# A two-layer hybrid decoder trunk in float32: the MLP's first product with its weights standing still, for 13 of 16 chunks

## The reference, cut to what matters

```python
def hybrid_layer(x, c_act, ...):
    mod = c_act @ ada_w + ada_b                 # 2048 -> 6 * 2048
    sh_a, sc_a, gt_a, sh_m, sc_m, gt_m = jnp.split(mod[:, None, :], 6, axis=-1)
    ...                                         # mixers, x = x + gt_a * (o @ w_out)
    h = rms_norm(x, norm_mlp) * (1.0 + sc_m) + sh_m
    u = jnp.square(jax.nn.relu(h @ mlp_w1))     # 256 x 2048 by 2048 x 8192
    return x + gt_m * (u @ mlp_w2)              # 256 x 8192 by 8192 x 2048
```

## Time and profile before

| what | value |
|---|---|
| median of 3 runs (lowest, highest) | 2588.86 us (2587.51, 2595.3) |
| profiled execution, its own time | 2593.14 us |
| its span, first to last instruction | 2591.1 us |
| mean granted TensorE clock | 0.977 |
| MLP of layer 1, supers 1 to 3 | 2043 to 2577 us of the span |
| MLP of layer 0, supers 1 to 3 | 819 to 1370 us |
| HBM read | 629.85 MB, 244 GB/s over the span |

### The profile page before, as it was taken

One profiled execution on the slowest core, in us unless ns is written; L12 is line 12 of the kernel. 1 busy time (PEld: TensorE's weight loads), 2 busy tenths in 40 slices (PEclk: granted clock), 3 DMA queues, 4 the chain that ended last, 5 costly groups with the idle time before them and its releaser, 6 DMA issues.

```text
span 2591.1 us, 29622 instructions
## 1 busy us (share of the span) xinstructions
PE 2403.2 (93%) x11276; PEld 1982.8 (77%) x11276; DVE 1789.3 (69%) x2145; ACT 1183.6 (46%) x1602; POOL 19.3 (1%) x44
## 2 busy tenths in 40 slices
PE   2679899997999999999998998999899999999997
PEld 1567777775887888887887877887788888888886
DVE  6888877767877777778776777676567545545555
ACT  2244554443543544444544555454454454453453
POOL 1000000000000000000000000000000000000000
PEclk9899999998999999999999999999999999999999
DMA  8978776777988989989885787556577666666664
GB/s 301 323 266 275 256 259 212 231 248 246 327 292 305 304 287 317 306 299 309 296 292 190 249 276 253 165 186 219 151 239 261 188 185 193 190 185 195 184 190 138
DMA packets 318549, 633.91 MB, mean 245 GB/s; under 512 B 20365, under 2 KB 41289, under 8 KB 317769
## 3 DMA queue, kind: packets, MB, share of 16 engines
q1 hardware_dynamic: 314368, 625.49, 73.4%
q10 hardware_dynamic: 4040, 6.54, 0.7%
HBM read 629.85 MB, written 2.10 MB: 244 GB/s over the span
## 4 chain that ended last, share of the span: by engine, by line
PE 36%; issue 33%; DVE 18%; DMA 8%; ACT 4%; POOL 0%; ACTq 0%; DVEq 0%; POOLq 0%
PE acc L1500 8%; PE acc L1502 7%; PE acc L1501 7%; DVE ada_acc L998 7%; DMA ada_raw<-in_ada_w 7%; DVE w_lo L1039 5%; PE pair L1500 2%; PE pair L1502 2%; PE pair L1501 2%; ACT w_hi L675 2%; PE bank_T L1411 1%; DMA w_raw<-in_nsa_cmp_v_w 1%; PE bank_T L1373 1%; DVE ybuf L1153 1%; DMA w_raw<-in_nsa_cmp_k_w 1%
## 5 line engine op out<-in xcount | busy, mean ns | idle before, releaser
L1039 DVE TENSOR_TENSOR w_lo<-w_raw,w_hi 128x1024 fp32r<-128x1024 f32 (+3 forms) x828 | 979.9, 1192 | 399.8 <-ACT w_hi L675 398.0
L675 ACT ACTIVATE w_hi<-w_raw 128x1024 fp32r<-128x1024 f32 (+3 forms) x828 | 848.6, 1033 | 795.3 <-PE acc L1502 369.5
L1500 PE MATMUL acc<-w_hi,hT_hi 128*128 128x512 f32 (+3 forms) x1536 | 613.3, 399 | 56.2 <-DVE w_lo L1039 42.6
L1502 PE MATMUL acc<-w_lo,hT_hi 128*128 128x512 f32 (+3 forms) x1536 | 592.8, 386 | 0.0
L1501 PE MATMUL acc<-w_hi,hT_lo 128*128 128x512 f32 (+3 forms) x1536 | 592.7, 386 | 0.0
L998 DVE SCALAR_TENSOR_TENSOR ada_acc<-ada_raw,silu_c,ada_acc 128x1024 f32<-128x1024 f32 x300 | 384.1, 1280 | 113.9 <-DMA ada_raw<-in_ada_w 113.0
L1500 PEld LDWEIGHTS acc<-w_hi,hT_hi 128*128 128x128 f32 x1536 | 294.6, 192 | 121.7 <-issue 31.3
L1502 PEld LDWEIGHTS acc<-w_lo,hT_hi 128*128 128x128 f32 x1536 | 293.6, 191 | 57.1
L1501 PEld LDWEIGHTS acc<-w_hi,hT_lo 128*128 128x128 f32 x1536 | 294.9, 192 | 51.7 <-issue 1.2
L1500 PE MATMUL acc<-w_hi,uT_hi 128*128 128x512 f32 (+1 forms) x720 | 284.9, 396 | 3.5 <-DVE w_lo L1039 3.5
L1502 PE MATMUL acc<-w_lo,uT_hi 128*128 128x512 f32 (+1 forms) x720 | 280.3, 389 | 0.0
(11 more groups left out here) (240 smaller groups left out, 2029.2 us busy)
## 6 DMA issues: line engine op xcount, KB each, us to landing
w_raw<-in_mlp_w SPq DMA_DIRECT2D x512, 512.0 KB, 4.8
ada_raw<-in_ada_w SPq DMA_DIRECT2D x320, 512.0 KB, 5.0
w_raw<-in_w_in SPq DMA_DIRECT2D x112, 512.0 KB, 4.9
arena<-in_ada_w SPq DMA_DIRECT2D x64, 512.0 KB, 6.2
w_raw<-in_w_out SPq DMA_DIRECT2D x64, 512.0 KB, 5.0
w_raw<-in_nsa_cmp_k_w SPq DMA_DIRECT2D x32, 512.0 KB, 4.7
w_raw<-in_nsa_cmp_v_w SPq DMA_DIRECT2D x32, 512.0 KB, 4.8
w_raw<-in_w_in SPq DMA_DIRECT2D x16, 388.0 KB, 4.0
```

Source lines behind the costliest of these rows:

```text
L675: a.activation(w_hi[:, Q % RING, :, 0:n], w_raw[:, Q % RING, :, 0:n], ACT.Copy).then_inc(hi_done, 1)
L1039: v.tensor_tensor(w_lo[:, Q % RING, :, 0:n], w_raw[:, Q % RING, :, 0:n], w_hi[:, Q % RING, :, 0:n].bitcast(F32), ALU.subtract).then_inc(lo ...
L1500: pe.matmul(o, st_hi[:, kt + k, tok], wh, start=first and k == 0, stop=False)
L1502: mm = pe.matmul(o, st_hi[:, kt + k, tok], wl, start=False, stop=last and k == 1)
```

## The change

For the chunks (s,0) to (s,3), all but (0,0), (0,1) and (0,2), the roles in the first product are exchanged. 13 chunks a layer, so 26 chunks and 208 pieces. `product_turned` loads 128 columns of the weight tile as TensorE's stationary operand. `w_hi` meets `hT`, one tensor now in which the high and the low input of a row of tiles lie side by side: 512 columns, high by high in the left 256 and low by high in the right. `w_lo` meets only the high input: 256 columns, added to the left. A chunk is worked as two halves t of 256 hidden features, each with an accumulator of its own, so a turned chunk takes two of the three. The sums have features on partitions, and there is no turn.

At a chunk's end ScalarE copies the right halves to `ybuf` (`u_copy`), VectorE adds the left halves from PSUM (`u_sum_halves`), ScalarE does relu, square and the rounding to `uT_hi` (`u_act`), VectorE the low part (`u_low`). The copies and additions stand at the second piece after the chunk's last, the rest at the second to fifth (two later in super 0). TensorE raises `u_pair` from the last matmul of half 0; for half 1 it waits for its own `piece_used` and then raises it. The core of the diff:

```diff
-def acc_of(chunk):
-    return CHUNKS[chunk][3] if type(chunk) is str else (8 * chunk[0] + chunk[1]) % 3
+def turned(chunk):
+    return type(chunk) is not str and chunk[1] < 4 and chunk not in ((0, 0), (0, 1), (0, 2))
...
+        for key in [chunk + (0,), chunk + (1,)] if turned(chunk) else [chunk]:
+            ACC_OF[l, key] = CHUNKS[key][3] if type(key) is str else turn_no % 3
...
+    for s in range(SUPERS):
+        for j in range(4):
+            if turned((s, j)):
+                done = 64 * s + 8 * j + 7
+                for t in range(2):
+                    side(M + done + 2, ("usum", l, s, j, t), 0)
+                    side(M + done + 2 + t + 2 * (s == 0), ("uact", l, s, j, t), 3)
+                    side(M + done + 4 + t + 2 * (s == 0), ("ulo", l, s, j, t), 3)
...
-        hT_hi, hT_lo = sb("hT_hi", [P, KT, SEQ], F32R), sb("hT_lo", [P, KT, SEQ], F32R)
+        hT = sb("hT", [P, KT, 2, SEQ], F32R)
+        hT_hi, hT_lo = hT[:, :, 0, :], hT[:, :, 1, :]
...
+            def u_copy(l, s, j, t):
+                n = U_NO[l, s, j, t]
...
+                act.wait_ge(u_pair, n + 1)
+                a.activation(u_half(j, t), acc[ACC_OF[l, (s, j, t)]][:, :, 256:512], ACT.Copy).then_inc(u_copied, 1)
+
+            def u_act(l, s, j, t):
+                n = U_NO[l, s, j, t]
+                act.wait_ge(u_sum, n + 1)
+                a.activation(u_half(j, t), u_half(j, t), ACT.Relu).then_inc(u_own, 1)
+                act.wait_ge(u_own, 2 * n + 1)
+                a.activation(u_half(j, t), u_half(j, t), ACT.Square).then_inc(u_own, 1)
+                act.wait_ge(u_own, 2 * n + 2)
+                kt = 4 * j + 2 * t
+                a.activation(uT_hi[:, kt:kt + 2, :], u_half(j, t), ACT.Copy).then_inc(v_hi, 1)
...
+            def u_sum_halves(l, s, j, t):
+                n = U_NO[l, s, j, t]
+                dve.wait_ge(u_copied, n + 1)
+                v.tensor_tensor(u_half(j, t), acc[ACC_OF[l, (s, j, t)]][:, :, 0:256], u_half(j, t), ALU.add
+                                ).then_inc(u_sum, 1)
+                dve.wait_ge(u_sum, n + 1)
+                dve.sem_inc(acc_free[ACC_OF[l, (s, j, t)]], 1)
+
+            def u_low(l, s, j, t):
+                kt = 4 * j + 2 * t
+                dve.wait_ge(v_hi, split_value(l, f"u{s}_{2 * j + t}"))
+                v.tensor_tensor(uT_lo[:, kt:kt + 2, :], u_half(j, t), uT_hi[:, kt:kt + 2, :].bitcast(F32), ALU.subtract
+                                ).then_inc(split_done, 1)
...
+            def product_turned(Q):
+                l, chunk, p = PIECES[Q]
+                pe.wait_ge(lo_done, Q + 1)
+                for t in range(2):
+                    key = chunk + (t,)
+                    if p == 0 and ACC_USE[l, key]:
+                        pe.wait_ge(acc_free[ACC_OF[l, key]], ACC_USE[l, key])
+                    for f in range(2):
+                        o = acc[ACC_OF[l, key]][:, f, :]
+                        for k in range(2):
+                            kt, cols = 2 * p + k, slice(P * (2 * t + f), P * (2 * t + f) + P)
+                            pe.matmul(o, w_hi[:, Q % RING, k, cols], hT[:, kt, :, :].rearrange("p a t -> p (a t)"),
+                                      start=p == 0 and k == 0, stop=False)
+                            mm = pe.matmul(o[:, 0:SEQ], w_lo[:, Q % RING, k, cols], hT_hi[:, kt, :], start=False,
+                                           stop=p == 7 and k == 1)
+                    if p == 7 and t == 0:
+                        mm.then_inc(u_pair, 1)
+                mm.then_inc(piece_used, 1)
+                if p == 7:
+                    pe.wait_ge(piece_used, Q + 1)
+                    pe.sem_inc(u_pair, 1)
```

More of the change, by code:

```diff
@@ L80 @@
 assert len(PIECES) == ALL
-def acc_of(chunk):
-    return CHUNKS[chunk][3] if type(chunk) is str else (8 * chunk[0] + chunk[1]) % 3
-LAST_PIECE, ACC_USE = {}, {}
-uses = [0, 0, 0]
+def turned(chunk):
+    return type(chunk) is not str and chunk[1] < 4 and chunk not in ((0, 0), (0, 1), (0, 2))
+LAST_PIECE, ACC_OF, ACC_USE = {}, {}, {}
+uses, turn_no = [0, 0, 0], 0
 for Q, (l, chunk, p) in enumerate(PIECES):
     if p == 0:
-        ACC_USE[l, chunk] = uses[acc_of(chunk)]
-        uses[acc_of(chunk)] += 1
+        if chunk == (0, 0):
+            turn_no = 0
+        for key in [chunk + (0,), chunk + (1,)] if turned(chunk) else [chunk]:
+            ACC_OF[l, key] = CHUNKS[key][3] if type(key) is str else turn_no % 3
+            turn_no += type(key) is not str
+            ACC_USE[l, key] = uses[ACC_OF[l, key]]
+            uses[ACC_OF[l, key]] += 1
     LAST_PIECE[l, chunk] = Q
@@ L231 @@
     side(M + 12, ("fill", l, "n2", 3), 0)
[L232 to L237, removed]
+    u_relu = {(0, 0): 22, (0, 1): 24, (0, 2): 29}
+    u_t = {(0, 0): (22, 23), (0, 1): (25, 26), (0, 2): (30, 31)}
     mlp_steps = []
@@ L345 @@
                                              "fq", "fk"]
-    for i, name in enumerate(names + [f"n2y{j}" for j in range(4)] + [(s, j) for s in range(SUPERS) for j in range(4)]):
+    for i, name in enumerate(names + [f"n2y{j}" for j in range(4)] + [(0, j) for j in range(3)]):
         slot = i % 2 if i < len(names) else (i - len(names)) % 2
@@ L469, in trunk @@
         v_hi, split_done = sem("v_hi"), sem("split_done")
+        u_pair, u_copied, u_sum, u_own = sem("u_pair"), sem("u_copied"), sem("u_sum"), sem("u_own")
         x_done, x_squared = sem("x_done"), sem("x_squared")
@@ L503, in acc_out @@
         def acc_out(l, chunk):
-            return acc_free[acc_of(chunk)], ACC_USE[l, chunk] + 1
+            return acc_free[ACC_OF[l, chunk]], ACC_USE[l, chunk] + 1
         def split_value(l, name):
@@ L808, in evac @@
             def evac(l, name):
-                a_ = acc[acc_of(name)]
+                a_ = acc[ACC_OF[l, name]]
                 if name == "fv":
@@ L889, in after @@
                         relu(l, step[2], step[3])
+                    elif kind == "usum":
+                        u_copy(l, step[2], step[3], step[4])
+                    elif kind == "uact":
+                        u_act(l, step[2], step[3], step[4])
                     elif kind == "square":
@@ L1315, in after @@
                         diagonals(l, step[2])
+                    elif kind == "usum":
+                        u_sum_halves(l, step[2], step[3], step[4])
+                    elif kind == "ulo":
+                        u_low(l, step[2], step[3], step[4])
                     elif kind == "resid":
@@ L1579, in _ @@
                     t_in(l, what)
-                if PIECES[Q][1] == "cw1":
+                if turned(PIECES[Q][1]):
+                    product_turned(Q)
+                elif PIECES[Q][1] == "cw1":
                     compress(Q)
```

36 lines of the change are left out of this document (22 added, 14 removed).

## The result

| | before | changed |
|---|---|---|
| median of 5 runs (lowest, highest) | 2588.86 us (2587.51, 2595.3) | 2606.5 us (2603.84, 2615.49) |
| profiled execution, span | 2593.14, 2591.1 us | 2606.5, 2604.5 us |

The ratio is 1.0075, 95% interval 1.0056 to 1.0094: 0.75% slower, where no difference was forecast and 2606 was the range's end. Run again in a later batch it gave 1.0077 (1.0058 to 1.0096).

The account below looks back on a forecast made before the run. TensorE's queue was taken as the bound, in layer 0 until VectorE or DMA takes over. Terms -25.2 + 11.0 + 10.9 + 5 = +1.7 us gave 2590.6, told as 2591 us; range for 8 in 10: 2578 to 2606.

Parts of the forecast that it names:

- Transposes: TensorE's queue, 26 first-product chunks: the transposes go, 0.97 us a chunk, -25.2 us in all.
- Shape: 208 turned pieces: 8 matmuls of 512 and 8 of 256 columns, 2.774 instead of 2.720 us each, +11.0 us.
- The self-wait: End of each turned chunk: TensorE waits for its own last matmul, 0.42 us a time, +10.9 us; bounds 4 to 14.
- ScalarE's chain: ScalarE's chunk-end work: about 2.7 us extra a chunk, `w_hi` still in time with 0.7 us to spare, 0 in layer 1.
- VectorE: Layer 0's turned chunks: additions fit but leave nothing to make up late landings, 0.4 us a chunk, +5 us; bounds 0, +16.
- rival B: Layer 0's first product: VectorE becomes the bound, additions and low halves ahead of `w_lo`, +16 us, 2605; chance 0.24.
- Accumulators: A turned chunk takes two of three: free in layer 1, in layer 0 part of the 0.4 us a chunk for VectorE.
- The sign for layer 1: Layer 1's turned chunks: the forecast is wrong if they differ from 22.6 us by over 0.3 us.
- the one for layer 0 against layer 1: The two MLPs: the forecast is wrong if layer 0's gains or loses over 10 us against layer 1's.

Follow-up runs that it names:

- e4: The changed kernel with only the matmul order 512, 256, 512, 256 columns made 512, 512, 256, 256: 2600.41 us.
- g2: The changed kernel without TensorE's self-wait and in order 512, 512, 256, 256, with ScalarE's relus and squares of turned chunks left out: 2584.82 us.
- h1: The changed kernel without self-wait, in order 512, 512, 256, 256, ScalarE's relu, square, rounding and the low parts one or two pieces later in supers 1 to 3: 2585.94 us.
- f4: The changed kernel without self-wait and in order 512, 512, 256, 256, with VectorE's additions of the left halves left out: 2590.03 us.
- f3: The changed kernel without self-wait, in order 512, 512, 256, 256, with copies and additions put behind the ada tile in the side list: 2619.42 us.
- h2: The changed kernel without self-wait, in order 512, 512, 256, 256, with relu and square as one VectorE instruction instead of ScalarE's: 2585.85 us.

## Why the prediction was wrong

1. *Transposes.* Right: 25.2 forecast, 27.8 measured.
2. *Shape* failed, by 7 us. The line through 280 and 512 columns gave 2.774 us a piece and the fast kind is 2.773. This is partly luck: in fast pieces a 512-column matmul takes 0.232 us, not 0.227, and a 256-column one 0.115, not 0.12 (and less than the floor of 0.117 that I had put under a stream of loads). What failed is that one length was taken for all pieces: most chunks ran at 2.827, 0.107 over the 2.720 of before, twice the term of 0.053. About 17 slow chunks make 7 us more. What the kind hangs on physically stays open; that the order 512, 512, 256, 256 ends it is shown. Of the Trainium skill's two rules (TensorE: Matmul & The Clock Gate, back-to-back issue gap and LDWEIGHTS), the gap of N/2.4 + 2.5 ns came out too small (worked out from it, an estimate, a pair takes 325 ns; measured 347 and 353). The 107 ns load is not contradicted: two short matmuls in a row, each with a load, start 115 ns apart in e4.
3. *The self-wait.* Right in kind, 0.42 taken, 0.54 measured in place and 0.58 alone. I had carried over ScalarE's 0.17 us between a result and the next instruction; TensorE took 0.27 to the load. 3 us more.
4. *ScalarE's chain* was the step whose mechanism failed, by some 7 us: "0.7 us to spare, so 0 in layer 1" held there, and layer 0 was never asked; I put it at nothing without a reason. The times of the chain were right (`w_hi` of d+3 and d+4 done at T + 3.7 and 6.5, forecast 3.8 and 6.8). But layer 0 needs the chunks of the first product to win back a lead over TensorE, 2.0 to 4.8 us before, and with the chain in front of the weights' rounding they don't. g2 (the chain without relu and square) and h1 (the same chain, later) show it. A slip beside it: by its own rows the extra work is 4.98 - 3.49 = 1.5 us a chunk, not 2.7, and the page shows 26.5 us more for 26 chunks, 1.0 each. Moving the same work later was enough to win the time back (h1).
5. *VectorE*: 5 forecast, about 3 found (f4, not clear of noise). The place was wrong: TensorE waits for `w_lo` in the second product, not at d+5 and d+6 of the turned one. That the chunks of the first product repair what the others lose was right, but I gave the loss of it to VectorE. The 1.8 us that I held against rival B were the waits with `acc` alone; with `pair` they are 2.4.
6. *Accumulators*: free as the order stands; f3 shows the price if it doesn't.

Forecast +1.7. With the sizes found, -25.2 + 11 + 7 + 14 + 9 = +16, as the two MLPs grew by 12.6 + 3.4. This agreement proves nothing, since 9 is what was left over in layer 0; what bears the 9 is g2, h1 and h2, and 7 and 3 us for ScalarE and VectorE make 10. The profiled spans differ by 13.4, because the front happened to be 2.7 shorter, the medians by 17.6; the changed kernel's own runs spread from 2603.84 to 2615.49. That 2606 is near rival B's 2605 is luck. B put it all on VectorE in the first product; about half of it lies in layer 0 beyond TensorE's terms, and of that VectorE has the smaller part. The sign for layer 1 came true (23.15 us is more than 0.3 from 22.6); the one for layer 0 against layer 1 just did not (9.2 us, not 10).

## What to carry to other kernels

Where one engine's queue is the bound, an own wait in it costs the drain plus the restart every time, 0.54 to 0.58 us here: let the reader wait for the last result itself. Split the end of a tile into what must be done at once (to empty the accumulator) and what can stand behind the next tile's preparation. And work out an engine's slack in the stretch with the least slack, not in the clean one: 0.7 us was plenty in layer 1 and a loss in layer 0. Where one stretch of a loop loses its lead and another wins it back, work added to the second is paid in the first.

## What the runs showed of the hardware

An alternation of 512- and 256-column matmuls, each with its own weight load, ran at two paces, 0.347 and 0.353 us a pair. In layer 1 a chunk kept the one that it started with; in layer 0 a stop of TensorE changed it at times, and the same kernel had 9 slow chunks of 13 in one execution and 13 in another. 512, 512, 256, 256 ran at one, 0.348. Matmuls of 512 columns alone went at 0.227 in every kernel where nothing stopped them (second-product chunks of 21.76 us).
